# Two-layer encoder trunk on one core: a third Strassen block per feed-forward, third weight sums by adding DMA, joins on ScalarE, lists ordered anew

## What is computed

```python
def _swiglu(h, w_gate, w_up, w_down):
    return (jax.nn.silu(h @ w_gate) * (h @ w_up)) @ w_down
...
    for l in range(DEPTH):
        x = x + 0.5 * _swiglu(_rms_norm(x, ffn1_norm[l]), ffn1_w_gate[l], ffn1_w_up[l], ffn1_w_down[l])
        h = _rms_norm(x, mix_norm[l])
        proj = h @ w_in[l]
...
        x = x + y @ w_out[l]
        x = x + 0.5 * _swiglu(_rms_norm(x, ffn2_norm[l]), ffn2_w_gate[l], ffn2_w_up[l], ffn2_w_down[l])
```

## Time and profile before

| what | value |
|---|---|
| three runs | 1024.97, 1027.45, 1025.89 us, median 1025.89 |
| the profiled execution | 1025.66 us, its span 1023.9 us |
| matmuls | 4905 |
| data moved | 208.99 MB, mean 204 GB/s |
| HBM read | 192.90 MB |

### The profile page before, as it was taken

One profiled execution on the slowest core, in us unless ns is written; L12 is line 12 of the kernel. 1 busy time (PEld: TensorE's weight loads), 2 busy tenths in 40 slices (PEclk: granted clock), 3 DMA queues, 4 the chain that ended last, 5 costly groups with the idle time before them and its releaser, 6 DMA issues.

```text
span 1023.9 us, 13331 instructions
## 1 busy us (share of the span) xinstructions
PE 1018.2 (99%) x4905; PEld 853.9 (83%) x4905; DVE 846.4 (83%) x1008; ACT 660.8 (65%) x836; POOL 330.8 (32%) x258
## 2 busy tenths in 40 slices
PE   9999999999999999999999999999999999999998
PEld 6888888998888888888888888889988888888887
DVE  6999977698976898888679889866999678988972
ACT  6767665576874575766557666647778556666761
POOL 2999400138850100000049990001589300000000
PEclk9999999999999999999999999999999999999999
DMA  8968578555544596748749574975366365947491
GB/s 278 309 191 277 162 209 274 160 185 176 207 161 128 182 328 183 244 140 234 228 154 339 166 226 135 274 248 174 127 214 226 123 173 185 331 140 233 158 240 42
DMA packets 175185, 208.99 MB, mean 204 GB/s; under 512 B 64112, under 2 KB 129936, under 8 KB 175120
## 3 DMA queue, kind: packets, MB, share of 16 engines
q1 hardware_dynamic: 173904, 206.03, 64.9%
q10 hardware_dynamic: 1216, 2.11, 0.7%
HBM read 192.90 MB, written 1.05 MB: 189 GB/s over the span
## 4 chain that ended last, share of the span: by engine, by line
PE 98%; ACT 1%; DVE 1%; DMA 0%; issue 0%; POOL 0%; ACTq 0%
PE bank L829 30%; PE bank L831 30%; PE bank L830 30%; PE bank L966 1%; PE bank L1128 1%; PE bank L1137 1%; PE bank L1158 1%; PE bank L868 0%; PE bank L1136 0%; PE bank L1160 0%; PE bank L836 0%; DMA cacc<-in_ffn_norm 0%; DVE htok L1902 0%; DVE x L1950 0%; ACT htok L1357 0%; PE bank L1146 0%
## 5 line engine op out<-in xcount | busy, mean ns | idle before, releaser
L1854 DVE TENSOR_TENSOR wlo<-raw,whi 128x2048 fp32r<-128x2048 f32 (+2 forms) x136 | 308.9, 2283 | 21.0 <-ACT whi L1344 21.0
L1344 ACT ACTIVATE whi<-raw 128x2048 fp32r<-128x2048 f32 (+2 forms) x160 | 302.9, 1910 | 25.3 <-DMA raw<-in_ffn_w_down 16.5
L829 PE MATMUL bank<-whi,hThi 128*128 128x512 f32 (+1 forms) x816 | 316.1, 387 | 0.0
L831 PE MATMUL bank<-whi,hTlo 128*128 128x512 f32 (+1 forms) x816 | 311.4, 382 | 0.0
L830 PE MATMUL bank<-wlo,hThi 128*128 128x512 f32 (+1 forms) x816 | 311.3, 381 | 0.0
L697 POOL TENSOR_TENSOR small<-small,expo 128x1 f32<-128x1 f32 (+3 forms) x20 | 30.0, 1505 | 470.5 <-DVE small L1895 432.9
L831 PEld LDWEIGHTS bank<-whi,hTlo 128*128 128x128 f32 x816 | 153.2, 188 | 29.6
L829 PEld LDWEIGHTS bank<-whi,hThi 128*128 128x128 f32 x816 | 153.3, 188 | 28.8
L830 PEld LDWEIGHTS bank<-wlo,hThi 128*128 128x128 f32 x816 | 153.4, 188 | 28.4
L829 PE MATMUL bank<-whi,gThi 128*128 128x512 f32 (+1 forms) x416 | 162.3, 390 | 0.0
L831 PE MATMUL bank<-whi,gTlo 128*128 128x512 f32 (+1 forms) x416 | 161.2, 388 | 0.0
(11 more groups left out here) (201 smaller groups left out, 1359.0 us busy)
## 6 DMA issues: line engine op xcount, KB each, us to landing
raw<-in_ffn_w_down SPq DMA_DIRECT2D x88, 512.0 KB, 4.7
raw<-in_ffn_w_gate SPq DMA_DIRECT2D x68, 512.0 KB, 4.2
raw<-in_ffn_w_up SPq DMA_DIRECT2D x68, 512.0 KB, 5.2
raw<-in_w_in SPq DMA_DIRECT2D x48, 512.0 KB, 4.9
htok<-in_ffn_w_gate SPq DMA_DIRECT2D x16, 512.0 KB, 6.1
heads<-in_ffn_w_up SPq DMA_DIRECT2D x16, 512.0 KB, 6.8
raw<-in_w_out SPq DMA_DIRECT2D x16, 512.0 KB, 4.6
raw<-in_w_in SPq DMA_DIRECT2D x8, 544.0 KB, 5.2
```

The costliest lines, as they stand in the source:

```text
L829: nc.tensor.matmul(out, lh, rh, start=start, stop=False, skip_group_check=skip)
L831: return nc.tensor.matmul(out, ll, rh, start=False, stop=stop, skip_group_check=skip)
L1344: nc.scalar.activation(whi[:, slot(u, RING), 0:USED[u]], src, ACT.Copy).then_inc(whi_ready, 1)
L1854: nc.vector.tensor_tensor(wlo[:, slot(u, RING), 0:n], src, whi[:, slot(u, RING), 0:n].bitcast(F32), ALU.subtract).then_inc(wlo_ready, 1)
```

## The change

- `BLK` is (2, 5, 8): three blocks in each feed-forward, over the chunks 2, 3 and 5, 6 and 8, 9. The plain chunks are 0, 1, 4, 7 and 10. PE's list is `first`, `strassen(2)`, `pair(4)`, `strassen(5)`, `pair(7)`, `strassen(8)`, `last`.
- The sum T3 is made by POOL: two DMAs with `accum_op` add the lower half of the up weights, read from HBM once more, to `chain[1]`, after the sum T1 of the same block, which reads it. DVE's `add_T3` is gone.
- The joins of the chunks 1 to 7 are made by ACT (`act_join`); DVE keeps those of 0, 8 and 9.
- The lists of SP, ACT and DVE are written anew for this. PE's waits use new tables.

```diff
-BLK = (4, 7)
+BLK = (2, 5, 8)
...
-UPPER = (1, 3, 6, 9)
-SUM = {"T1": 1, "T2": 1, "T3": 1, "T4": 1}
+UPPER = (1, 4, 7, 10)
+SUM = {"T1": 1, "T2": 1, "T3": 32, "T4": 1}
...
+            def add_rows(l, f, c, name):
+
+                done = per_block(l, f, c)
+                if name == "T3":
+                    pool.wait_ge(chain_landed[1], done * 32)
+                    pool.wait_ge(sum_ready["T1"], done)
+                    dst, src = chain[1], quarter_of(wu[f], l, c, 1)
+                dst = dst.rearrange("p (k n) -> p k n", k=4)
+                for k in (0, 2):
+                    nc.gpsimd.dma_start(dst[:, k:k + 2, :], src[:, k:k + 2, :],
+                                        accum_op=ALU.add).then_inc(sum_ready[name], 16)
+
+            def sums(l, f):
+
+                add_rows(l, f, 2, "T3")
+                add_rows(l, f, 5, "T3")
+                add_rows(l, f, 8, "T3")
+
             for l in range(DEPTH):
                 norm(l, 0)
+                sums(l, 0)
...
                 norm(l, 2)
+                sums(l, 1)
...
-                pair(2)
-                pair(3)
-                strassen(4)
-                pair(6)
-                strassen(7)
-                pair(9)
+                strassen(2)
+                pair(4)
+                strassen(5)
+                pair(7)
+                strassen(8)
                 last()
...
+                def act_join(c):
+
+                    act.wait_ge(turned_landed, per_turn(l, f, c) * 16)
+                    if c:
+                        act.wait_ge(glo, per_ffn(l, f, c - 1, 1))
+                    nc.scalar.activation(g_turned.bitcast(U16).rearrange("p (n b) -> p b n", b=2),
+                                         turned.rearrange("p (b j) r -> p b (j r)", b=2), ACT.Copy).then_inc(joined, 1)
...
-                def add_T3(c):
-                    dve.wait_ge(sum_ready["T1"], per_block(l, f, c) * SUM["T1"])
-                    add(c, "T3", lower_raw(c, "B22"))
-
...
                 mixed_rows()
-                gate_split(2, 1)
                 join(0)
+                of_chain(2, "B11")
+                rest_joined(0)
+                add_T1(2)
                 down_split(0)
+                of_chain(2, "T1")
                 mul(1, 0)
                 mul(1, 1)
-                rest_joined(0)
+                add_T2(2)
                 mixed_rest()
```

More of the change, by code:

```diff
@@ L1523, in first @@
                         silu(0, 1)
-                        split(0, 4)
                         factors(1)
@@ L1574, in ffn @@
+                sum_of(5, "T2")
+                lower(5, "B22")
+                keep(5, 0, "B11")
+                lower(5, "B21")
                 split_planes(4, 0)
-                block_silu(4, 1)
                 split_planes(4, 1)
+                sum_of(5, "T3")
+                keep(5, 1, "T1")
+                sum_of(5, "T4")
                 down_split(4)
-                first_of(7, "B11")
+                keep(5, 2, "T2")
+                gate_split(7, 0)
+                act_join(4)
@@ L2118, in ffn @@
-                down_split(1)
-                of_chain(4, "B11")
-                mul(2, 1)
-                rest_joined(1)
-                add_T1(4)
+                of_chain(2, "T2")
+                lower(2, "B22")
+                lower(2, "B21")
+                add_T4(2)
+                of_chain(2, "T3")
+                of_chain(2, "T4")
+                rest_joined(1)
+                down_split(1)
+                gate_first(2)
+                up_second(2)
+                up_first(2)
@@ L2147, in ffn @@
-                gate_split(6, 1)
+                add_T2(5)
+                mul(4, 0)
+                mul(4, 1)
+                of_chain(5, "T2")
+                lower(5, "B22")
+                add_T4(5)
+                lower(5, "B21")
+                of_chain(5, "T3")
+                of_chain(5, "T4")
+                gate_first(5)
                 down_split(4)
-                join(4)
-                of_chain(7, "B11")
-                add_T1(7)
+                up_first(5)
                 rest_joined(4)
+                up_second(5)
@@ L2177, in ffn @@
-                gate_split(9, 1)
+                mul(7, 0)
+                mul(7, 1)
+                of_chain(8, "T2")
+                lower(8, "B22")
+                add_T4(8)
+                lower(8, "B21")
+                of_chain(8, "T3")
+                of_chain(8, "T4")
                 down_split(7)
-                join(7)
+                up_first(8)
+                gate_split(10, 0)
+                up_second(8)
+                gate_first(8)
                 rest_joined(7)
-                gate_split(10, 0)
```

237 lines of the change are left out of this document (104 added, 133 removed).

## The result

The changed kernel takes 1054.2 us (median of 4 runs, 1051.86 to 1055.42), the kernel before beside it 1025.4 us: 1.0275 times as long, 95% interval 1.026 to 1.0289. Forecast were 1052.0 us, range 1034 to 1086.

What follows compares the result with a forecast made beforehand. PE, 98% of the chain, was taken as the bound; -10.9 matmuls + 13.5 first blocks + 2.6 tail + 20 POOL's order + 1.5 restart = +26.7, from 1025.66 to 1052 us, range 1034 to 1086.

Steps and rivals of the forecast that it cites:

- the two kinds of places: PE idle near the first block (four places, 2 to 5 us) and at chunk 10's small transpose (two, some 10 us).
- The matmuls: PE, all four feed-forwards: one more block in each saves 48 matmuls of 0.227 us, 10.9 us less.
- The load of DVE and ACT: Busy time rises to 871 us on DVE and 721 on ACT; neither the bound on average, both late in places.
- The first block: Block at chunk 2: PE waits 4.5 us in the first feed-forward, 3 in each other; 13.5 us, ends 5 and 30.
- The 0.5 in chunk 1: In the feed-forwards after the first, chunk 1's second half comes 0.5 us late, the mixed rows 1.4 more.
- The order on POOL: Rotary steps behind block 8's adding DMAs delay tile 0's norm root; PE loses 10 us in both layers, 20 us.
- 82: Upper end for POOL's order: the steps keep a loaded DVE's pace throughout, 41 us a layer.
- The restart of PE: PE may be granted less clock after 10 us of idling: 0 to 4 us, taken as 1.5.
- The tail: Behind block 8, the mul of chunk 10 comes 1.3 us late, twice: 2.6 us, ends 0 and 6.
- The adding DMA: POOL's DMAs for T3 land in 6.8 to 20 us; up to 16 hidden, taken as hidden; 20 costs 4 a block.
- the adding DMA was not slow enough to matter: Rival on T3's sum: adding DMAs land in 20 us, 48 us on top, 1100 us; chance 0.10.
- the first rival: Lists keep up, POOL in time if steps average under 1.4 us: 1015, up to 1022 us; chance 0.09.

Runs made afterwards that it cites:

- Run 7: The changed kernel with DVE's split of B11 of block 2 put ahead of the join of chunk 0 in each feed-forward: 1053.55 us.
- run 9: The changed kernel with DVE's and ACT's lists around the first block reordered (B11, sum T1, then join; chunk 1's muls behind T2 and B22): 1047.43 us.
- run 3: The changed kernel with 8 rotary steps on POOL between the adding DMAs of blocks 5 and 8, 28 behind, nothing else: 1039.83 us.
- run 10: Run 9's lists with run 3's POOL order and two small moves, against the changed kernel: 1033.07 us; with chunk 0's join on ACT too, 1032.42 us.
- run 1: The changed kernel with POOL's rotary steps dealt between adding DMAs: ten ahead of block 5's, eighteen ahead of block 8's, eight behind: 1078.62 us.
- run 2: The changed kernel with twelve rotary steps on POOL between the adding DMAs of blocks 5 and 8, the other 24 behind: 1055.07 us.
- Run 4: The kernel before (blocks 4 and 7, its lists) with third sums by POOL's adding DMAs ahead of the rotary steps, DVE's left out: 1025.22 us.
- run 8: The changed kernel with the rest of the mixed rows ahead of the sum T2 on DVE: 1065.08 us.
- run 6: The changed kernel with the joins of chunks 1 to 7 back on DVE, each ahead of its rest: 1075.32 us.

## Why the forecast was right

The sign, the range and the two kinds of places were right, and the total missed by 2 us. That closeness is luck: the first blocks cost 8 us more than forecast and POOL's order 9 less. Their order was wrong with it: the forecast had POOL's order as the largest loss, and it is 14.2 us with its slow matmuls against 21.5 at the first blocks.

**The matmuls**, -10.9: 48 fewer, at 0.227 us. Right. A kernel without the waits was not reached, so the saving shows only as a term of the sum.

**The load of DVE and ACT**: 871 and 721 forecast, 871.0 and 725.2 measured. The 4 us on ACT are the joins. I took its 1024-element uint16 copy of 1.06 us for them; in the changed kernel's groups ACT's join reads 1.37, with its interleaved words, where DVE's reads 0.76:

```profile
L1522 ACT ACTIVATE gates<-qkT 128x1024 uint16<-128x1024 uint16 x28 | 38.3, 1368 | 13.6 <-DMA qkT<-qkT 13.5
...
L2016 DVE COPY gates<-qkT 128x1024 uint16<-128x1024 uint16 x12 | 9.1, 761 | 12.0 <-DMA qkT<-qkT 12.0
```

**The first block**, 13.5 forecast, 21.5 measured, 20.2 without the slow matmuls. This term was mis-sized, and the step that failed is "Counted along DVE's list": the count ran the join right behind the mixed rows at its own length, 0.65 us, and left out that its input is a DMA. DVE idled 2.86 us there in the first feed-forward and 2.24 to 2.39 in the others. B11's split began at 33.91 instead of 30.8, and PE waited 3.77 us for it where I had it in time; PE was there at 32.40, too, not at 32.9. In the other three I had 2 us from DVE and 1 for ACT; they lost 4.4. The 0.5 in chunk 1 and the wait for the mixed rows at T1, 1.6 us instead of 1.4, came as counted; not counted were 1.6 to 1.7 at the down of chunk 0, whose split stands behind the join. Run 7 shows that the join alone is not the cause of the whole (without it ahead the wait moves on); run 9, which takes it out of the way and orders what follows by who waits, got back 6.8. The rest of the miss is ACT, idle behind the same join (run 7), which the count of DVE's list alone could not see.

**The order on POOL**, 20 forecast, 11.2 of waits measured, 5.25 and 5.93. Runs 3 and 10 confirm the mechanism, to within 1 us of what PE's rows hold. Its two estimates were both off. The pair of DMAs took 7.8 us from release to the next instruction (125.5 to 133.3), not 3: 5 us later. The steps took 54.0 us (133.3 to 187.3), not 60.8: 22 of the 36 were done when DVE's residual ended at 179.24, not 13. The two errors go against each other, and the second is the larger: the root came 4.4 us before the end that the feed-forward would have had, where I had it 0.4 behind. The sum T1 itself was in time to 2 us (released 66 us before the end that the feed-forward would have had, forecast 64). The fast pace of 0.555 us a step was right, and its start was right to 1 us: it sets in at 177.98, with DVE's residual, which reads PSUM, and not at that operation's end.
The sentence on the Trainium skill holds as far as it went: the pace was back as soon as DVE stopped, so 20 was nearer than 82. But with 13 steps from the kernel before, the loaded pace was taken as a constant, and as the slowest stretch of it, 3.7 us a step; the mean of all 36 steps there, 2.6 us, would have given 19. Ten steps took 53 us in run 1, twelve 42 us in run 2, 22 took 46 us in the change. The Trainium skill (SBUF — State Buffer, Who interferes with whom) says that a VectorE operation with two inputs in SBUF contends with a GpSimd operation that reads SBUF, and that one with at most one such input, outside the two-port modes, does not. The traces agree: 2.08 us in the median beside the first kind, 0.33 at most beside operations with an input from PSUM (run 1).

**The restart of PE**, 1.5 forecast, 4.3 measured: 1.3 behind the wait of 3.77 us, 1.4 and 1.6 behind the two at the transpose. I expected it at the two long waits only and without a row to price it. It is a part of what each long wait costs: a quarter to a third on top.

**The tail**, 2.6 forecast, 0.9 measured: 0.69 us of wait in the second feed-forward of layer 0, none that shows in layer 1. **Small waits**, about 3, had no term: 0.1 to 0.3 us, most where an operand comes just in time.

**The adding DMA**, hidden: right, but by less than the forecast's reading had it. It took the 6.8 us of the earlier trace rows for a pair, where they are one DMA's; the third sum is complete 13 to 18 us after T1's, against the bound of 16 to 20, and ACT does wait for it. Run 4 measures no cost (0.9998, 0.9989 to 1.0007) with two blocks.

The rivals: the lists did not keep up (waits of DVE's splits in all four feed-forwards), the adding DMA was not slow enough to matter, and the condition that I gave for the first rival, under 1.4 us a step, was nearly met: 1.5. But that mean holds 14 steps at the fast pace beside a DVE that stood still. With the pair issued in 3 us instead of 7.8, the steps before those would have gained the 4.8 us, two to four steps more at 1.3 to 2.1 us each, and the root, by this estimate, would have come only 1 to 2 us sooner, where PE waited 5.1. And the first blocks alone would still have made the kernel slower (run 3: 1.0135).

## What to carry to other kernels

An idle stretch ahead of a late instruction is cover that something is using: before an operation that waits is put ahead of it in the same queue, count what must still run behind the wait, at the pace of that stretch, and look for the split that leaves both readers in time; here 0, 12 and 8 steps ahead of the wait gave 1054, 1055 and 1040 us. When counting along a loaded engine's list, give every operation the landing of its input as well as its length, look what the engine behind it stands still for meanwhile, and put first what another engine still has to work on. A saving on the engine that is the bound is worth only what the engines that feed it can follow: 10.9 us of matmuls brought 21.5 us of waits and slow matmuls behind an engine that was 83% busy before and after.

## What the runs showed of the hardware

- The second of two adding DMAs issued back to back from POOL is held until about when the first has landed. The group of these DMAs in the changed kernel: 12 pairs, the second of each held by no semaphore that the profile shows, and a landing of 6.1 us.

```profile
  issue: 77.3, 12
...
DMA to landing us min/median/max: 5.7/6.1/10.8
```

  77.3 us over 12 is 6.4 us a pair, in which POOL did nothing else; single ones read 4.9 to 10.0, and they follow the first one's landing: issued at 39.64, 81.33 and 126.08, it landed after 6.0, 10.8 and 6.2 us, and the second left at 45.94, 92.52 and 132.57. So a sum made of two such DMAs is complete 12 to 17 us after the first issue, not 6.
- POOL's small operations beside a loaded DVE have no fixed price: they wait while DVE reads both inputs from SBUF, for several of its operations in a row if these follow each other without a gap (nine in run 1), and go at full pace beside one that reads PSUM. A CAST of 128 x 2 elements read 0.19, 0.69, 2.4 and 17.95 us in four kernels; sixteen multiplications of the same size 18.05, 20.51 and 12.11.
- In the traces of the change and of the runs, every wait of PE of 3.4 us or more behind the first 20 us was followed by slow matmuls, 4 to 13 of 512 columns at 0.43 us, half speed; in the change's windows the granted clock read 0.66 to 0.75 there. Behind waits of up to 1.7 us the matmuls ran at 0.227 at once. Between the two the same wait went either way in one kernel: in run 8 one of the four waits of 3.2 us was followed by slow matmuls and three were not, in run 7 two of three of 2.3, in run 6 one of four of 2.0. So the length of the wait alone does not decide it.
- A transposing DMA has no fixed price beside weight loads: 3.0 to 8.1 us to landing in the kernel before, with a median of 3.4, and the one that the first block waits for took 4.9 there and 6.87 in the change.
